# First block of a three-layer transformer kernel: when w_ada's quarter-slabs are loaded and used, how the mixer's groups are normed, and how the out projection and the layer norms' sums are done

## The reference, cut to what matters

```python
mod = silu(c) @ w_ada + b_ada                     # 1024 x 6144, one vector
sh1, sc1, g1, sh2, sc2, g2 = split(mod, 6)
mix = token_mixer(x * (1 + sc1) + sh1, ...)       # below
x = layer_norm(ALPHA * x + g1 * mix, ln1_g, ln1_b)
ff = swiglu(x * (1 + sc2) + sh2, w_gate, w_up, w_down)
x = layer_norm(ALPHA * x + g2 * ff, ln2_g, ln2_b)
```

## Time and profile before

| what | us |
|---|---|
| median of 3 runs | 1181.86 (1181.27 to 1183.54) |
| the profiled execution's own time | 1181.6 |
| its span | 1179.8 |
| PE busy | 1100.8 (93%) |
| DVE, ACT, POOL busy | 727.6, 556.7, 198.6 |
| mean granted clock of PE | 0.97 |

### The profile page before, as it was taken

The page is one execution under the profiler, slowest core; times in us unless marked ns, Lnnn a source line. Parts: engine busy times, 40 slices in busy tenths (PEclk is TensorE's granted clock), DMA queues, the critical chain, the costliest instruction groups (busy, mean ns, idle before and its releaser), DMA issues.

```text
span 1179.8 us, 20647 instructions
## 1 busy us (share of the span) xinstructions
PE 1100.8 (93%) x8093; PEld 1013.6 (86%) x8093; DVE 727.6 (62%) x1154; ACT 556.7 (47%) x958; POOL 198.6 (17%) x225
## 2 busy tenths in 40 slices
PE   6996699899999989988999999998997899999998
PEld 6684479699999968887999999997875699999998
DVE  5674346667755447765765645576768675655564
ACT  1412262654444366633554534475546664544453
POOL 0000000033330010101133330122210023332011
PEclk9897799899999999998999999998999999999999
DMA  9825434376655525430465555654432056553661
GB/s 356 300 102 214 142 143 161 126 250 218 209 148 168 175 81 206 169 118 1 144 214 174 182 148 161 198 207 143 143 143 72 1 193 200 177 192 110 197 215 37
DMA packets 183348, 192.79 MB, mean 163 GB/s; under 512 B 5801, under 2 KB 143314, under 8 KB 183154
## 3 DMA queue, kind: packets, MB, share of 16 engines
q1 hardware_dynamic: 182272, 191.15, 48.0%
q0 software_dynamic: 144, 0.52, 0.1%
q10 hardware_dynamic: 866, 0.21, 0.1%
HBM read 190.83 MB, written 1.05 MB: 163 GB/s over the span
## 4 chain that ended last, share of the span: by engine, by line
PE 75%; DVE 13%; DMA 5%; ACT 5%; issue 2%; POOL 0%; SPq 0%; DVEq 0%; ACTq 0%; POOLq 0%
PE gemm L1845 20%; PE gemm L1847 20%; PE gemm L1846 20%; PE gemm L2038 4%; DVE wlo L1230 3%; DMA part<-in_w_ada 3%; PE gemm L2000 1%; ACT whi L823 1%; PE aux L1949 1%; PE aux L2265 1%; PE aux L1963 1%; DVE xlo L1256 1%; DMA raw<-in_w_ada 1%; DMA raw<-in_gla_w_in 1%; DVE neg_max L1805 1%
## 5 line engine op out<-in xcount | busy, mean ns | idle before, releaser
L1230 DVE TENSOR_TENSOR wlo<-raw,whi 128x1024 fp32r<-128x1024 f32 (+2 forms) x328 | 372.0, 1181 | 101.7 <-ACT whi L823 101.1
L1845 PE MATMUL gemm<-ohi,whi 128*128 128x256 f32 x1408 | 400.5, 284 | 5.1 <-DVE olo L1256 3.9
L1847 PE MATMUL gemm<-ohi,wlo 128*128 128x256 f32 x1408 | 395.6, 281 | 0.0
L1846 PE MATMUL gemm<-olo,whi 128*128 128x256 f32 x1408 | 394.7, 280 | 0.0
L823 ACT ACTIVATE whi<-raw 128x1024 fp32r<-128x1024 f32 (+2 forms) x328 | 291.9, 957 | 66.5 <-PE gemm L1847 55.2
L1845 PEld LDWEIGHTS gemm<-ohi,whi 128*128 128x128 f32 x1408 | 266.8, 189 | 11.2 <-DVE olo L1256 6.6
L1846 PEld LDWEIGHTS gemm<-olo,whi 128*128 128x128 f32 x1408 | 266.7, 189 | 1.1 <-issue 0.8
L1847 PEld LDWEIGHTS gemm<-ohi,wlo 128*128 128x128 f32 x1408 | 266.6, 189 | 0.0
L1845 PE MATMUL gemm<-acthi,whi 128*128 128x256 f32 x528 | 147.9, 280 | 0.0
L1847 PE MATMUL gemm<-acthi,wlo 128*128 128x256 f32 x528 | 147.5, 279 | 0.0
L1846 PE MATMUL gemm<-actlo,whi 128*128 128x256 f32 x528 | 147.2, 279 | 0.0
(11 more groups left out here) (347 smaller groups left out, 1505.2 us busy)
## 6 DMA issues: line engine op xcount, KB each, us to landing
raw<-in_ffn_w_in SPq DMA_DIRECT2D x44, 1024.0 KB, 6.8
raw<-in_ffn_w_out SPq DMA_DIRECT2D x32, 704.0 KB, 5.5
part<-in_w_ada SPq DMA_DIRECT2D x28, 512.0 KB, 5.3
raw<-in_gla_w_in SPq DMA_DIRECT2D x6, 2048.0 KB, 7.8
raw<-in_diff_w_in SPq DMA_DIRECT2D x6, 2048.0 KB, 7.7
raw<-in_w_gate SPq DMA_DIRECT2D x11, 1024.0 KB, 5.0
raw<-in_w_up SPq DMA_DIRECT2D x11, 1024.0 KB, 7.4
raw<-in_w_down SPq DMA_DIRECT2D x16, 704.0 KB, 5.8
```

The costliest lines, as they stand in the source:

```text
L1230: dve.tensor_tensor(wlo[hslot][:, q * w:(q + 1) * w], raw[slot][:, q * w:(q + 1) * w], whi[hslot][:, q * w:(q + 1) * w].bitcast(F32), ALU. ...
L1845: pe.matmul(dst, st_hi, mv_hi, start=start, stop=False)
L1846: pe.matmul(dst, st_hi, mv_lo, start=False, stop=False)
L1847: return pe.matmul(dst, st_lo, mv_hi, start=False, stop=stop_)
```

## The change

1. Slab 6 becomes quarters as well, 32 quarters in all, and `load_late` and PE's 64 one-column matmuls are gone. Quarters are used in the heads: 6 and 7 at the end of head 0, then 8; 9, 10; 11; 12, 13; 14, 15; 16, 17; 18, 19 at the ends of heads 1 to 7. 20 to 23 stand beside the out projection's first slab, 24 to 31 in gate_up0. The loads hang behind in_hc (4 to 7), in_gb (8 to 13), the out slabs (14 to 19, 20, 21) and gate_up0.
2. The groups are normed in place (`mixed`), squares of pair 0 are taken in head 5, its root in head 6, its norm and high part in head 7.
3. PE opens the out projection without filler, k tiles 0, 1, 4, 5 for all four tiles of the slab first, then modulation 8, then k tiles 6, 7, 2, 3. The second slab is done tile by tile.
4. GpSimd adds res and its squares for tiles 0 to 6 (`layer_sums`), at out0 and at down0. PE then adds one sum and the last tile, two matmuls for each bank instead of eight.

```diff
-PART_SLABS = (4, 5, 7, 8, 9, 10, 11)
+PART_SLABS = tuple(range(4, 12))
...
             behind = {("ada1", 0): [load_x], ("in_q", 0): [*parts(0, 1), load_const, *parts(2, 3)],
-                      ("in_hc", 0): parts(4, 5), ("in_gb", 0): [*parts(6, 7), load_late, *parts(8, 9)],
-                      ("out0", 0): parts(10, 11, 12, 13), ("gate_up0", 0): parts(14, 15),
-                      ("gate_up0", 1): parts(16, 17, 18, 19), ("gate_up0", 2): parts(20, 21),
-                      **{("gate_up0", i): parts(18 + i) for i in range(4, 10)}, ("gla_z", 0): [load_gates]}
+                      ("in_hc", 0): parts(4, 5, 6, 7), ("in_gb", 0): parts(8, 9, 10, 11, 12, 13),
+                      ("out0", 0): parts(14, 15, 16, 17, 18, 19), ("out0", 1): parts(20, 21), ("gate_up0", 0): parts(22, 23, 24, 25),
+                      **{("gate_up0", i): parts(23 + i) for i in range(3, 9)}, ("gla_z", 0): [load_gates]}
...
+            def layer_sums(name):
+                n = me.n.get(ln_sq_ready.name, 0)
+                for t in range(1, KT - 1):
+                    pool.wait_ge(dve_read, FIRST_RES[name] + t + 1)
+                    me.again()
+                    me.did(pool.tensor_tensor(mean[:, :], tl(res, 0) if t == 1 else mean[:, :], tl(res, t), ALU.add))
+                    pool.wait_ge(ln_sq_ready, n + t + 1)
+                    ins = pool.tensor_tensor(sq_sum[:, :], tl(ln_sq, 0) if t == 1 else sq_sum[:, :], tl(ln_sq, t), ALU.add)
...
             def beside_head(i):
                 if i in (4, 5):
                     split_all("out0", None, range(2 * i - 8, 2 * i - 6))
+                if i == 5:
+                    group_squares(0, attn_ready, 2)
                 if i == 6:
-                    group_squares(0, attn_ready, 2)
-                if i == 7:
                     group_root(0, G[0])
                     group_squares(2, gated_ready, 2)
+                if i == 7:
+                    high_parts(0, 1)
+                    group_root(2, G[1])
...
+            group_squares(3, gated_ready, 4)
+            high_parts(4, 5)
             take_pair(3)
             group_squares(1, attn_ready, 4)
...
+            PARTS_OF_HEAD = ((6, 7), (8,), (9, 10), (11,), (12, 13), (14, 15), (16, 17), (18, 19))
...
+                if i == 7:
+                    mix_norm(0, 1)
+                for n in PARTS_OF_HEAD[i]:
+                    modulate_part(n)
+            mix_low(0, 1)
+            mix_norm(4, 5)
+            mix_low(4, 5)
+            mix_norm(6, 7)
+            mix_norm(2, 3)
+            mix_low(6, 7, 2, 3)
+            dve.wait_ge(mod_done, 9)
...
-                if i == 1:
-                    modulation(5)
+                if i in (2, 4, 6):
+                    modulation({2: 5, 4: 6, 6: 7}[i])
                 if i == 5:
-                    modulation(7)
+                    group_stats((0,), C("blk"), mix_sq, G[0:1])
                 if i == 6:
-                    group_stats((0,), C("blk"), mix_sq, G[0:1])
-                if i == 7:
                     group_stats((2,), C("blk"), mix_sq, G[1:2])
             values(NH - 1)
-            pe.wait_ge(late_in, 16)
-            columns_by_c(6, late, range(0, 2), 0, None)
-            group_stats((1, 3), C("blk"), mix_sq, (X[1], X[0]))
-            columns_by_c(6, late, range(2, KT), 0, KT - 1).then_inc(mod_done, 1)
+            group_stats((3, 1), C("blk"), mix_sq, X[0:2])
...
+            OUT_ORDER = (0, 1, 4, 5, 6, 7, 2, 3)
+            pe.wait_ge(lo_ready, 4 * (PH["out0"].j0 + 1))
+            out_columns(0, range(4), OUT_ORDER[0:4], True, False)
+            modulation(8)
+            out_columns(0, range(4), OUT_ORDER[4:8], False, True)
             banks.claim(X[3], mod_read)
...
+            pe.wait_ge(lo_ready, 4 * (PH["out0"].j0 + 2))
+            for t in range(4):
+                out_columns(1, (t,), OUT_ORDER, True, True)
+                if t == 1:
+                    modulation(9)
+            first_sums()
...
-            keep_warm(X[2], 2)
-            gemm("out0", dve_read, olo_from=8, order=(0, 1, 4, 5, 2, 3, 6, 7), after=beside_out0)
...
-                def before(at):
-                    if k == 0 and at.it is None and at.i == KT - 1:
-                        mean_sums(range(KT - 2))
...
                     if at.i == KT - 1:
-                        mean_sums([KT - 2])
+                        first_sums()
```

More of the change, by code:

```diff
@@ L136, in plan @@
         Phase("in_kv", 1, 8 * KV, 0, 1, by="kv", ahead=False, slot=0),
-        Phase("in_q", 1, SLAB, 4, 1, ahead=False, slot=1), direct("in_gc", 0), direct("in_hc", 1), direct("in_gb", 0), ada(6),
+        Phase("in_q", 1, SLAB, 4, 1, ahead=False, slot=1), direct("in_gc", 0), direct("in_hc", 1), direct("in_gb", 0),
         Phase("out0", 2, SLAB, 4, 1, slot=1), *ffn(0),
@@ L525, in build @@
         sources = {
-            **{f"ada{i}": columns(ada, 512 * i) for i in (0, 1, 6)},
+            **{f"ada{i}": columns(ada, 512 * i) for i in range(2)},
             "in_q": columns(w_in, 0), "in_kv": kv_slab,
@@ L756, in _ @@
                            a["p_2"].rearrange("l b (t p) n -> p l (b t) n", p=P)).then_inc(p_in, 16)
+            layer_sums("down0")
             skip_squares("gla_z")
@@ L994, in _, with high_parts @@
             group_root = lambda g, bank: roots([(bank, tl(mix_sq, 2 * g, 2))], 1.0 / HD, 0)
+            def high_parts(*tiles):
+                for t in tiles:
+                    me.next(norm_ready)
+                    me.did(act.activation(tl(ohi, t), tl(mixed, t), ACT.Copy), ohi_ready)
             def beside_head(i):
@@ L1015, in _ @@
                     take_pair(i // 2 - 1)
+            group_squares(3, gated_ready, 4)
+            high_parts(4, 5)
             take_pair(3)
             group_squares(1, attn_ready, 4)
-            group_squares(3, gated_ready, 4)
-            group_root(2, G[1])
-            prep(order=(0, 1), free=PH["in_gb"].tile0 + 4)
+            group_root(3, X[0])
             group_root(1, X[1])
[L1022 to L1026, removed]
+            high_parts(6, 7, 2, 3)
             square0 = tile_square(FIRST_RES["out0"])
@@ L1426, in group_make, with mix_norm, mix_low @@
                 return make
-            mix_make = group_make(mixed, mix_sq, lambda t: A("attn_norm_g", t) if t < 4 else A("conv_norm_g", t - 4))
+            def mix_norm(*tiles):
+                for t in tiles:
+                    if t % 2 == 0:
+                        me.next(sd_ready)
+                    gain = A("attn_norm_g", t) if t < 4 else A("conv_norm_g", t - 4)
+                    me.did(dve.scalar_tensor_tensor(tl(mixed, t), tl(mixed, t), gain, tl(mix_sq, t), ALU.mult, ALU.mult),
+                           norm_ready)
+            def mix_low(*tiles):
+                for t in tiles:
+                    me.next(ohi_ready)
+                    me.did(low_part(t, tl(mixed, t), ohi, olo), olo_ready)
             def masked_maxima(i):
@@ L1943, in keep_warm @@
                     pe.matmul(bank[:, 0:moving.shape[1]], ones[:, :], moving, start=True, stop=True)
[L1945 to L1952, removed]
             def modulation(i):
                 if i < 4:
+                    src = raw[i] if i < 2 else early[i - 2]
                     pe.wait_ge(landed[i] if i < 2 else early_in[i - 2][1], 16)
-                    columns_by_c(i, raw[i] if i < 2 else early[i - 2], (KT - 2, KT - 1), KT - 2, None)
+                    for k in (KT - 2, KT - 1):
+                        for m in range(4):
+                            pe.matmul(X[3][:, 4 * i + m:4 * i + m + 1], src[:, 512 * k + P * m:512 * k + P * (m + 1)],
+                                      c_act[:, k:k + 1], start=k == KT - 2 and m == 0, stop=False, skip_group_check=True)
                     pe.wait_ge(dve_summed, i + 1)
@@ L2149, in layer_norm @@
             def layer_norm():
-                mean_sums(range(KT - 1, KT))
+                pe.wait_ge(dve_read, STREAM[0] + KT)
+                pe.matmul(X[0][:, 0:T], ones[:, :], tl(res, KT - 1), start=False, stop=True)
+                me.next(ln_sq_ready, KT)
+                pe.matmul(X[1][:, 0:T], ones[:, :], tl(ln_sq, KT - 1), start=False, stop=True).then_inc(mean_done, 1)
             OPERANDS = [8]
             STREAM = [banks.n[dve_read.name]]
-            banks.claim(X[3], mod_read)
@@ L2199, in between @@
                     if at.i == KT - 1:
-                        mean_sums([KT - 2])
-                gemm(f"down{k}", dve_read, shape="down", before=before, after=between)
+                        first_sums()
+                gemm(f"down{k}", dve_read, shape="down", after=between)
             def ple(k):
```

102 lines of the change are left out of this document (48 added, 54 removed).

## The result

The kernel with the change takes 1167.5 us (median of four runs, 1163.6 to 1169.6) against 1182.7 for the kernel before beside it; the ratio is 0.9864, with a 95% interval of 0.9840 to 0.9887. That is 15 us faster. The prediction was 25.6 us, with 16 to 35 in its range: the sign was right, the size was not. The profiled executions stand 12.0 us apart (1181.6 and 1169.6).

The account below looks back on a forecast made before the run. PE, 93% busy, was held up some 11 us at each of two late quarters. Gains of 23.2 to the first norm and 2.4 in down0 made 25.6 us, from 1181.6 to 1156.0; range 1147 to 1166.

Parts of the forecast that it names:

- The two old waits: Heads 0 and 4: PE idle some 11 us each for a late quarter; both go, projection 0 ending 12.3 ahead.
- Heads 1 to 3: New stall of 1.1 us before head 1's transposes, none in head 2; projection 3 ends 11.2 us ahead.
- The wait for the out slab: Heads 4 and 5: ACT waits from 118.5 to 125.1; PE stalls 3.5 us, then 2.3 at group sums.
- The fall of the clock: From head 5, after the out slab wait: group sums, scores and projection 6 run slow, 2.7 us back.
- From the heads to the out projection: After projection 7: one-column products and filler gone, stalls 2.2 and 2.1; out projection opens 8.2 us later, 26.0 ahead.
- The second clock fall: Around the out projection's opening: group sums and first of the 48 products at half rate, 2.9 us back.
- The out projection: Up to the first layer norm: 5.2 us of sums gone, stalls of 1.8, 1.5 and 3.2 added; 2.8 won.
- GpSimd's additions: Out projection, tiles 5 and 6: four last additions at 0.74 us each, PE waits 3.2; 1.15 kept for the range.
- down0: Before the second norm: 5.2 us of PE's sums go, last residual waits behind low parts; 2.4 us gained.
- The clock did not hold: Rival: clock holds once or twice in the thin stretches; gain 28.3 to 31.2 us, 1150.4 to 1153.3; chance 0.24.
- The rival of larger stalls: Rival: larger stalls inside the heads, with late quarters and slow additions; 9.6 us less gain, 1165.6; chance 0.20.
- The slower rival, through gate_up0: Rival: slabs 4 to 10 stand behind late-used quarters and cost 28 us in seven bodies, 1184.0; chance 0.04.

Follow-up runs that it names:

- e3: Kernel before with only the load order changed: quarters 6 to 9 issued ahead of the slabs that held them; 1161.9 us, ratio 0.9805.
- e4: Changed kernel with ACT's split of the first out slab moved from heads 4 and 5 to heads 5 and 6; 1162.4 us, ratio 0.9834.
- e10: Changed kernel with ACT taking pair 3 and pair 1's squares ahead of high parts 4 and 5; 1163.1 us, ratio 0.9836.
- e9: Changed kernel with ten filler products on PE: before head 5's transposes, values 7 and the last group sum; 1163.9 us, ratio 0.9838.
- e6: Changed kernel with the first layer norm's sums back on PE, down0's still on GpSimd; 1167.8 us, ratio 0.9867.
- e8: Changed kernel with the second out slab's first two low quarters ahead of DVE's wait for modulation 8; 1165.3 us, ratio 0.9857.
- e7: Changed kernel with down0's sums back on PE, the first norm's still on GpSimd; 1168.2 us, ratio 0.9875.
- e11: Changed kernel with later out-slab split, earlier squares, both norms' sums on PE, earlier slab 1 low quarters and six filler products; 1152.1 us, ratio 0.9753.

## Why the prediction was wrong in size

- **The two old waits: right.** Their removal brings 22 us alone (e3). Head 0's logits came 1.76 us after in_gc's end; 89.5 was forecast where in_gc ends at 87.7, the same distance. But the profile came to that point 3.8 us later than the one of before. My sum stood on one execution, and the range had no term for this.
- **Heads 1 to 3: right.** Projection 3 ended 25.6 us after in_gc's end against 25.05 in the forecast; the stall before head 1's transposes was 1.4, not 1.1.
- **The wait for the out slab: right in place and in sum.** ACT waited 6.81 (6.5 forecast). PE's part was 3.88 and 1.12 instead of 3.5 and 2.3. The fall of the clock was forecast at 2.7 and cost 3.4: projection 6 5.43 instead of 3.65 (I took the 4.80 of a projection that had been cold for only part of its length), the sum 2.04 instead of 1.10, the scores 0.7 more. Idle time and clock together were 8.5 in the forecast and 8.4 in the trace. Moving the split (e4) wins back 5 to 7 of them.
- **From the heads to the out projection: the step that failed first.** The stall before the last sum, "stall 2.1, since high parts 4 and 5 wait for DVE", was 4.08, because quarter 19 was costed as a quarter alone, 3.5 us, while SP issues a 2 MB slab 1 us behind it: 5.64, and 4.92 to 6.16 in six more profiles with the same order. e10 shows that this order on ACT was worth about 4 us. The second clock fall was forecast and came; e9 puts it at about 2, the forecast at 2.9.
- **The out projection: the step that failed second.** "2.8 won here" was the sum of PE's products less three stalls. In the trace the stretch is 1.4 us longer than before. By its rows it goes at DVE's pace: DVE idles 4.72 us for modulation 8 and then has slab 1's low parts, four quarters and the residuals ahead of it, and its quarters take up to 1.89 instead of 1.54 us beside GpSimd. e6 gives PE its products back and the stretch becomes 1.1 to 1.8 shorter, e8 gives DVE its work earlier and it becomes 0.7 to 1.4 shorter; in the total times neither stands out of the noise, so how much of the shortfall is DVE's queue stays an estimate from the traces. The forecast followed PE from stall to stall and gave DVE a place only in three of them; it never added up DVE's own queue.
- **GpSimd's additions.** The four last ones took 0.72 to 0.75 us, as taken, and PE waited 1.8 for them instead of 3.2. The first four took 1.03 to 1.19, beside DVE. The rule of the Trainium skill ("GPSIMD Engine Reference", 1. Specifications), that GpSimd contends with DVE instructions of two SBUF inputs, is borne out here: beside those additions the quarters' instructions, which have both inputs in SBUF, took up to 1.21 us instead of 0.75, and back at 0.75 in e6 without them. What I left out is that DVE slows down as well, on the engine that set the pace. The residuals, which I had named as such instructions, read one input from a matmul's bank and stayed at 0.48 us in both.
- **down0: forecast 2.4, nothing came.** The mechanism, residual behind low parts, is in the rows above. gla_q landed 8.7 us after its issue, its first high part started 1.3 us before PE's last product instead of 2.6, and the last sums ran at half rate, 1.0 more: together the 2.2 that are missing. I had taken the load of before, whose first high part started 7.7 us after the issue; it is 8.8 and 8.9 in the changed kernel, and 7.8 in e7, with the sums back on PE. And I had counted PE's saved work and not that its clock falls in the 4 us of waiting.
- **The rivals.** The clock did not hold. The rival of larger stalls gave 1165.6 and came nearest, with a late quarter and slow additions among its causes. The slower rival, through gate_up0, did not show: the stretch from norm to norm is as long as before.
- **From the second norm to g_z: a term put at nothing, 1.2 us.** The chain passes there through the load of a 2 MB slab, in flight for 7.94 us before and for 8.79 in the changed kernel. The stretch takes 27.2 to 27.7 us in the six profiles with all norm sums on PE, and 28.3 to 28.7 in the eight with GpSimd's sums in one place or in both (e6 and e7 have 28.3 and 28.4). So it goes with GpSimd's sums; by what way they would lengthen a load stays open.

## What to carry to other kernels

Where a change removes large waits and also reorders three engines, try the removal alone first: here two moved lines of a load list were worth 22 us, and the rest of the change lost some 6 of them; with its queues put right, filler in its waits and its GpSimd sums taken back, it gave 9 more. Work taken off the busiest engine counts only where no other engine is waited for next: down0's saved 5.2 us became a wait of 4 us, in which the clock fell, and the last four sums took 1.9 us instead of 0.86. So sum up the queue of every engine in a stretch, not only the stalls of the busiest. In an engine's list, put what needs nothing late (pair 1's squares, scaling of a head) ahead of what waits for a load (a slab's split, high parts behind a quarter): each of two such moves was worth 4 to 5 us by the medians.

## What the runs showed that I had not expected

- A quarter of 512 KB that lands in 3.5 us alone took 4.92 to 6.16 us in seven profiles in which a 2 MB slab was issued 1 us behind it on the same queue: it looks as if the later load took its share of the DMA engines at once, though no run moved the slab away to show it. A slab that took 7.7 us took 8.7 with one quarter issued 0.4 us ahead of it and another 3.4 us behind.
- GpSimd additions of 128x256 beside DVE instructions of two inputs took up to 1.19 us instead of 0.74, and these DVE instructions up to 1.21 instead of 0.75. Even a small one of 128x8 (L1521) took 0.70 beside GpSimd's last additions and 0.17 in e6 without them.
- 3.5 us of filler ahead of the transposes did not keep the clock up in e9: with PE idle for 0.44 and 1.97 us around it, it was 0.50 at 136 to 142 us. In e11, where PE's longest idle times in the heads were 1.39 us (at 100), 0.73 (at 90) and 0.42 (at 139), it held. In e3 it fell, at 152 us, with PE busy all the time on one-column products.
- The same instructions up to head 0 came to its logits up to 3.7 us apart in nine profiles, and those after g_z took from 723.6 to 728.7 us.
